# Half of the prompt's attention and output projection carried out inside the expert stage, with the second gather summed by token in column tiles

## The reference

```
mod = silu(c) @ w_ada + b_ada          -> shift, scale, gate, twice
h   = RMSNorm(x) * (1 + sc1) + sh1
q, k, v, p = split(h @ w_in)           # 512 features each
o_a = stick-breaking attention(q, k, v)    # 8 heads x 64, strictly causal
o_b = causal means over 2, 4, 8, 16 tokens of p, minus p, per-group map
x   = x + gt1 * RMSNorm(concat(RMSNorm(o_a), RMSNorm(o_b)) @ w_out)
h2  = RMSNorm(x) * (1 + sc2) + sh2
x   = x + gt2 * RMSNorm(PEER(h2))
PEER: per token and head (8 heads): two lists of 128 scores, the best 16
      of each, the best 16 of their 256 sums -> 16 of 16384 experts;
      sum over the 128 picks of gate * gelu(h2 . u_experts[i]) * v_experts[i]
```

## Time and profile before

| what | value |
|---|---|
| time, three runs | 3822.36, 3818.93, 3820.96 us |
| median | 3820.96 us |
| span of the profiled execution | 4199.6 us |
| mean granted clock of PE in it | 0.881 of full speed |
| expert stage in it | 904.6 to 4199.6 us |
| gathers | 2176 (1088 of each table) |

### The profile page before, as it was taken

How to read it: one execution, slowest core, us unless ns; L and a number is a source line. 1 busy time by engine, 2 the same in 40 slices (tenths; PEclk the granted TensorE clock), 3 DMA queues, 4 the chain that set the end, 5 groups by cost and what they waited for, 6 DMA issues and landing times.

```text
span 4199.6 us, 38180 instructions
## 1 busy us (share of the span) xinstructions
PE 3314.8 (79%) x9348; PEld 1593.5 (38%) x9348; DVE 2313.6 (55%) x5821; ACT 950.0 (23%) x2161; POOL 2152.0 (51%) x2222
## 2 busy tenths in 40 slices
PE   8998989928777777877777777777777777887677
PEld 2454555513333333333333333333333333333222
DVE  2104552867755665555665655566555665556442
ACT  1003773312221221112112211211121121112111
POOL 0000300236566665666666666566666665666665
PEclk9999999969898898898888888888888888888888
DMA  9104102159999999999999999899999999999997
GB/s 357 64 15 126 32 19 113 61 188 352 344 357 359 353 359 354 347 368 343 341 359 347 350 356 344 332 354 355 360 347 358 358 357 348 343 363 358 361 362 303
DMA packets 365168, 1245.51 MB, mean 297 GB/s; under 512 B 52129, under 2 KB 57505, under 8 KB 362751
## 3 DMA queue, kind: packets, MB, share of 16 engines
q0 software_dynamic: 313504, 1141.02, 72.4%
q1 hardware_dynamic: 48852, 96.77, 6.6%
q10 hardware_dynamic: 2576, 5.10, 0.4%
HBM read 1220.34 MB, written 22.39 MB: 296 GB/s over the span
## 4 chain that ended last, share of the span: by engine, by line
PE 38%; issue 17%; another core or an unknown queue 9%; DVE 5%; DMA 4%; POOL 3%; ACT 1%; DVEq 0%; POOLq 0%; ACTq 0%; SPq 0%
PE ps_y L1692 33%; PE ps_q L950 5%; DMA urow<-in_u_tab,idx 3%; POOL urow L1473 2%; POOL vrow L1473 1%; DMA vrow<-in_v_tab,idx 1%; DVE urow L1612 1%; ACT diag L1580 1%; DVE aux L993 0%; PE ps_s L961 0%; DVE i L996 0%; DVE sel L996 0%; DVE i L992 0%; DVE aux L1029 0%
## 5 line engine op out<-in xcount | busy, mean ns | idle before, releaser
L1692 PE MATMUL ps_y<-vrow,diag 128*128 128x512 f32 (+1 forms) x4352 | 2220.8, 665 | 647.5 <-issue 329.9
L1612 DVE CUSTOM_DVE_ANT_0 urow<-urow,ps_h 128x1024 f32<-128x1024 f32 x1088 | 1299.8, 1220 | 1025.2 <-DMA urow<-in_u_tab,idx 865.6
L1692 PEld LDWEIGHTS ps_y<-vrow,diag 128*128 128x128 f32 (+1 forms) x4352 | 884.3, 209 | 1893.6 <-issue 1576.9
L1473 POOL DMA_INDIRECT vrow<-in_v_tab,idx x1088 | 1031.6, 948 | 785.7 <-issue 287.4
L1473 POOL DMA_INDIRECT urow<-in_u_tab,idx x1088 | 1030.7, 947 | 430.5 <-issue 282.8
L1580 ACT ACTIVATE diag<-const,wgt 128x128 f32<-128x128 f32 x1024 | 373.1, 396 | 1766.2 <-PE ps_y L1692 643.3
L950 PE MATMUL ps_q<-aux,w_q_sb 128*128 128x128 f32 x2048 | 271.7, 292 | 58.1 <-issue 49.4
L950 PEld LDWEIGHTS ps_q<-aux,w_q_sb 128*128 128x128 f32 x2048 | 263.9, 207 | 94.4 <-issue 93.2
L1293 POOL TENSOR_TENSOR xo<-xo,ot 128x1024 f32<-128x1024 f32 (+1 forms) x9 | 21.1, 2343 | 352.2 <-DVE ot L1249 352.2
L530 PE MATMUL ps_z<-hT,w_in_sb 128*128 128x512 f32 (+1 forms) x576 | 190.5, 491 | 4.6 <-DVE hT L448 4.6
L625 POOL MEMSET kTs<- 128x384 f32 x1 | 0.4, 418 | 322.7 <-POOLq L344 322.7
(11 more groups left out here) (181 smaller groups left out, 2341.3 us busy)
## 6 DMA issues: line engine op xcount, KB each, us to landing
ada<-in_w_ada SPq DMA_DIRECT2D x12, 2048.0 KB, 12.5
urow<-in_u_tab,idx POOLq DMA_INDIRECT x1088
vrow<-in_v_tab,idx POOLq DMA_INDIRECT x1088
w_in_sb<-in_w_in SPq DMA_DIRECT2D x8, 1024.0 KB, 17.9
w_q_sb<-in_w_query SPq DMA_DIRECT2D x8, 1024.0 KB, 14.3
x<-in_x_p ACTq DMA_DIRECT2D x8, 512.0 KB, 6.6
w_out_sb<-in_w_out SPq DMA_DIRECT2D x8, 512.0 KB, 7.0
xo<-in_x_p SPq DMA_DIRECT2D x8, 512.0 KB, 3.7
```

The source lines that it names most:

```text
L1473: nc.gpsimd.indirect_dma_start(ring[k % RING][:, :], None, A[table][:, :], bass.IndirectOffsetOnAxis(ap=places[:, col:col + 1], axis=0)).t ...
L1612: nc.vector.tensor_tensor_reduce(out=urow[k % RING][:, :], in0=urow[k % RING][:, :], in1=ps_h[:, :], scale=1.0, scalar=0.0, op0=ALU.mult, ...
L1692: last = nc.tensor.matmul(ps_y[0:rows, c], diag[s % DIAGS][:, 0:rows], vrow[k % RING][:, c], start=(s == 0), stop=(s == PH * width(n) - 1))
```

## The change

The change does five things. The attention and output stages handle only queries and tokens 0 to 511 and the sample tokens: 11 units per pair and five tiles. The rest is in a class `Front`, cut into 102 "spots": 72 for attention (18 for each of four pairs: 16 units and two to drain the pipeline), then norms, eight products with halves of w_out, and ten for residual and second norm. A spot stands after a group of four picks in the expert stage on PE, ACT and DVE (`spot`; three a head in body 1, four a head in bodies 2 to 4, 14 of them in body 4), with its loads and stores on SP at the same place. Its tiles go through DRAM between the steps.

The v rows are gathered one token at a time (partition = pick, 128 picks of the token). Their indices and weights are transposed by PE. For four tokens, a "quad", ACT puts 128x4 weights into the middle column of four 63-column windows of zeros (`put`), and PE multiplies a 32-column view of each window with the token's rows, into 32 partitions of ps_y each (`quad`: eight products of 32x512). The v rows of a tile are gathered in the body after that of its u rows, so there are ten bodies. The first has u rows alone, the last v rows alone. The u ring has 6 buffers, the v ring 8, and POOL issues four u, then four v (two v in body 1). The search of a head is cut into 17 steps, one after each u product, and shares one PSUM bank with its queries. The bodies are unrolled.

```diff
-    for qc in range(2):
-        top = 4 * qc + 3
-        for kb in range(top, -1, -1):
-            c0 = max(0, kb * P - qc * 512)
-            for h in range(2):
-                units.append(dict(h=h, bank=qc, kb=kb, c0=c0, c1=512, first=kb == top, diag=kb >= 4 * qc,
-                                  last=kb == 0, opens=kb == top and h == 0, closes=kb == 0 and h == 1))
+    top = EARLY - 1
+    for kb in range(top, -1, -1):
+        for h in range(2):
+            units.append(dict(h=h, bank=0, kb=kb, c0=kb * P, c1=HALF, first=kb == top, diag=True,
+                              last=kb == 0, opens=kb == top and h == 0, closes=kb == 0 and h == 1))
     for kb in (2, 1, 0):
-        units.append(dict(h=2, bank=2, kb=kb, c0=0, c1=P, first=kb == 2, diag=kb == 2, last=kb == 0,
+        units.append(dict(h=2, bank=1, kb=kb, c0=0, c1=P, first=kb == 2, diag=kb == 2, last=kb == 0,
                           opens=kb == 2, closes=kb == 0))
...
+NU = NT + 1
+URING = 6
+VRING = 8
+ZRING = 4
...
-    tiles = TILES[-1:] + TILES[:-1]
+    tiles = TILES[-1:] + TILES[:EARLY]
...
-    heads = {2: [0], 3: [1], 4: [2], 5: [3], 6: [4], 7: [5], 8: [6, 7]}
...
+    PAIR, UNITS = 18, 16
+    ATT = 4 * PAIR
+    SQ = ATT + 1
+    OUT = (ATT + 8, ATT + 14)
+    POST = ATT + 20
+    END = POST + 10
...
+    def score(self, pe, m):
+        i, j, h, kb, diag, c0, lo = self.unit(m)
+        if m % self.UNITS == 0:
+            pe.wait_ge(self.kq_in, 32 * (i + 1))
+        if m >= 2:
+            pe.wait_ge(self.e_done, m - 1)
+        hr = slice(HD * h, HD * (h + 1))
+        self.nc.tensor.matmul(self.z[m % 2][:, c0:HALF], self.kT[hr, P * kb:P * (kb + 1)], self.q[hr, c0:HALF],
+                              start=True, stop=True, skip_group_check=True).then_inc(self.z_done, 1)
+    def after(self, pe, m):
+        i, j, h, kb, diag, c0, lo = self.unit(m)
+        z = self.z[m % 2]
+        pe.wait_ge(self.sp_done, m + 1)
+        last = self.nc.tensor.matmul(z[:, c0:HALF], self.ntri, self.sp[m % 2][:, c0:HALF], start=False, stop=True,
+                                     skip_group_check=True)
+        if j and lo < HALF:
+            last = self.nc.tensor.matmul(z[:, lo:HALF], self.nones, self.R[h][(j - 1) % 2][:, lo:HALF], start=False,
+                                         stop=True, skip_group_check=True)
+        last.then_inc(self.t_done, 1)
+    def values(self, pe, m):
+        i, j, h, kb, diag, c0, lo = self.unit(m)
+        if m % self.UNITS == 0:
+            pe.wait_ge(self.v_in, 16 * (i + 1))
+            if i:
+                pe.wait_ge(self.o_read, i)
+        pe.wait_ge(self.e_done, m + 1)
+        if diag:
+            pe.wait_ge(self.w_done, self.diags(m))
+        hr = slice(HD * h, HD * (h + 1))
+        self.nc.tensor.matmul(self.acc[hr, c0:HALF], self.v[:, kb, hr], self.w[m % 2][:, c0:HALF], start=(j == 0),
+                              stop=(kb == 0), skip_group_check=True).then_inc(self.pv_done, 1)
...
+    def logs(self, act, own, m):
+        i, j, h, kb, diag, c0, lo = self.unit(m)
+        nc, s = self.nc, self.sp[m % 2][:, c0:HALF]
+        act.wait_ge(self.z_done, m + 1)
+        if m >= 2:
+            act.wait_ge(self.t_done, m - 1)
+        own.link(nc.scalar.activation(s, self.z[m % 2][:, c0:HALF], ACT.Abs))
+        own.link(nc.scalar.activation(s, s, ACT.Exp, scale=-1.0))
+        nc.scalar.activation(s, s, ACT.Ln, bias=1.0).then_inc(self.l_done, 1)
...
+    def softplus(self, dve, own, m):
+        i, j, h, kb, diag, c0, lo = self.unit(m)
+        nc, s = self.nc, self.sp[m % 2]
+        own.wait()
+        dve.wait_ge(self.l_done, m + 1)
+        soft = nc.vector.scalar_tensor_tensor(out=s[:, c0:HALF], in0=self.z[m % 2][:, c0:HALF], scalar=0.0,
+                                              in1=s[:, c0:HALF], op0=ALU.max, op1=ALU.add)
+        if diag:
+            own.link(soft)
+            self.masked(s, c0).then_inc(self.sp_done, 1)
+        else:
+            soft.then_inc(self.sp_done, 1)
+        if kb:
+            dve.wait_ge(self.sp_done, m + 1)
+            if m >= 2:
+                dve.wait_ge(self.t_done, m - 1)
+            new, old = self.R[h][j % 2], self.R[h][(j - 1) % 2]
+            fresh = HALF if j == 0 else lo
+            if fresh > c0:
+                own.add(nc.vector.tensor_copy(new[:, c0:fresh], s[:, c0:fresh]))
+            if fresh < HALF:
+                own.add(nc.vector.tensor_tensor(new[:, fresh:HALF], old[:, fresh:HALF], s[:, fresh:HALF], ALU.add))
...
+        def spot(g, j):
+            if g < PH:
+                return None
+            if g < 2 * PH:
+                return 3 * (g - PH) + j - 1 if j else None
+            p = 3 * PH + 4 * (g - 2 * PH) + j
+            return p if p < front.END else None
...
         @block.gpsimd
...
-            def gather(table, ring, full, n, h, k):
-                col = width(n) * h + k
-                places = idx0 if is_sample(n) else idx
-                nc.gpsimd.indirect_dma_start(
-                    ring[k % RING][:, :], None, A[table][:, :],
-                    bass.IndirectOffsetOnAxis(ap=places[:, col:col + 1], axis=0)).then_inc(full[k % RING], 16)
...
-                    for k in range(TOPK):
-                        if ahead and k < width(un):
-                            pool.wait_ge(u_used, slots(un, uh) + (k - RING + 1))
-                            pool.sem_inc(pool_passed, 1)
-                            gather("u_tab", urow, u_full, un, uh, k)
-                        if k < width(n):
-                            if not (is_sample(n) and h == 0):
-                                pool.wait_ge(v_used, slots(n, h) + (k - RING + 1))
-                                pool.sem_inc(pool_passed, 1)
-                            gather("v_tab", vrow, v_full, n, h, k)
...
+            def gather_u(n, s):
+                k, at = u_slot(n, s) % URING, (find.idx0 if is_sample(n) else find.idx)[:, s:s + 1]
+                if s % width(n) == 0:
+                    pool.wait_ge(idx_ready, find.known(head(n, s // width(n))))
+                if u_slot(n, s) >= URING:
+                    pool.wait_ge(u_used, u_slot(n, s) - URING + 1)
+                nc.gpsimd.indirect_dma_start(urow[k][:, :], None, A["u_tab"][:, :],
+                                             bass.IndirectOffsetOnAxis(ap=at, axis=0)).then_inc(u_full[k], 16)
+            def gather_v(n, i):
+                t = token(n, i)
+                k, at = v_slot(n, i) % VRING, find.idxT[n % 2][:, t:t + 1]
+                if i == 0:
+                    pool.wait_ge(idxT_ready, n + 1)
+                if v_slot(n, i) >= VRING:
+                    pool.wait_ge(v_used, v_slot(n, i) - VRING + 1)
+                nc.gpsimd.indirect_dma_start(vrow[k][:, :], None, A["v_tab"][:, :],
+                                             bass.IndirectOffsetOnAxis(ap=at, axis=0)).then_inc(v_full[k], 16)
+            for b in range(BODIES):
+                nu = PH * width(b) if b < NU else 0
+                nv = rows(b - 1) if b else 0
+                for i in range(0, max(nu, nv), 4):
+                    each = 2 if b == 1 else 4
+                    for u in range(i, min(i + 4, nu)):
+                        gather_u(b, u)
+                    for v in range(i * each // 4, min(i * each // 4 + each, nv)):
+                        gather_v(b - 1, v)
...
-                            nc.scalar.activation(diag[s % DIAGS][:, :], ident, ACT.Copy, scale=weight)\
-                                .then_inc(diag_ready, 1)
...
+            def put(n, c):
+                q, j = n * QUADS + c, rows(n) // QUADS
+                if q >= ZRING:
+                    act.wait_ge(v_used, quad_end(q - ZRING))
+                nc.scalar.activation(place[:, q % ZRING, 0:j, MID],
+                                     wgtT[:, 0:rows(n)].rearrange("p (j c) -> p j c", j=j)[:, :, c], ACT.Copy)\
+                    .then_inc(placed, 1)
...
-                    un, uh = (n, h + 1) if h < PH - 1 else (n + 1, 0)
-                    if h < PH - 1 or more:
-                        products(un, uh)
-                    if h == 0:
-                        if not is_sample(n):
-                            finish(n - 1)
-                            find.search(own, dve, dve_passed, n, PH - 1)
-                    elif more:
-                        find.search(own, dve, dve_passed, n + 1, h - 1)
-                    if h < PH - 1 or more:
-                        weights(un, uh)
...
+            for b in range(NU):
+                w = width(b)
...
+                    g = head(b, h)
+                    early = 3 if h == 0 else 0
+                    if b and g + 2 < HEADS:
+                        for step in range(early):
+                            find.search(own, dve, g + 2, step)
+                    for k in range(w):
+                        product(b, h, k)
+                        if k == (1 if h == 0 else 2) and g:
+                            weights(g - 1)
```

(43 more changed lines are left out.)

1117 lines of the change are left out of this document (750 added, 367 removed).

## The result

The changed kernel takes 3875.66 us (median of four runs, 3868.83 to 3884.36) against 3821.66 us: 1.4% slower, ratio 1.0141 with a 95% interval of 1.0125 to 1.0158. The forecast was 3757, faster; the time lies inside the range, on the other side of zero, at the place that rival B gave (3880). The profiled span is 3872.7 us, 3 us from the median; the span of before, at 4199.6, had been 379 us above its median.

What follows compares the result with a forecast made beforehand. Gathers were taken to bound the expert stage, PE or its chains the stages before. Terms -225 + 60 + 14 + 25 + 10 + 15 + 10 + 27 = -64 took 3821 to 3757 us, range 3650 to 3900.

Steps and rivals of the forecast that it cites:

- rival B: Bodies 2 to 4 and last body: chain of waits starves gathers at 7.03 us a quad; 3978, middle 3880; chance 0.28.
- front: Stages before the experts: attention loses 16 units in four pairs, -170, output four tiles, -55; together -225 us.
- moved bytes, and what spots still hold up: Expert stage: 24.6 MB of moved attention and output transfers share full queues with the gathers at 410 GB/s, +60 us.
- body 1: Eight heads in the expert stage: DVE's 34.7 us a head against 30.7 of gathers, up to +32, taken as +25.
- spots of bodies 2 to 4, with output work: 72 attention spots at a period of 10.8 us, +10 for uneven arrival; output work among spots +15.
- last body: v rows alone, two quads in the ring: 11.9 us against 10.2 over 32 quads, +27, bounds 0 and 98.
- the signs that the prediction named: Softplus waiting over 2 us a spot for ACT, POOL behind u products: slower; front under 200 us or last body below 250 GB/s: wrong.
- ring of waits: Spots of bodies 2 to 4: DVE, POOL, PE and ACT wait in turn, 19.0 us and the quad for two groups.
- The quad, on which I let the outcome depend: Eight narrow products on PE, taken as 2.6 us between 1.75 and 7.03; the gain is gone at 3.8.
- Rival A: Expert stage stays gather-bound throughout, slack between 1.34 and 1.28 us a gather taking up small stalls: 3656 us; chance 0.18.
- Rival C: Expert stage's profiled dips are in timed runs too and come from the diagonals; quads bring 1.28 us a gather: 3625; chance 0.08.
- undisturbed pace of 1.28 us a gather: Expert stage of the kernel before: gathers at 1.28 us in an undisturbed stretch, timed runs at 1.34, 5% above.

Runs made afterwards that it cites:

- experiment 1: Changed kernel with a spot's work put ahead of the quad on PE and ahead of the weight copy on ACT: 3707.33 us, ratio 0.9702 to the kernel before.
- experiment 3: Changed kernel without spots and their transfers, tiles 5 to 8 taking h2 and x1 of tiles 1 to 4: 3631.68 us, ratio 0.9501 to the kernel before.
- experiment 4: Changed kernel with v rows going round twelve buffers in the last body, four of them from the u ring: 3823.24 us, ratio 1.0001 to the kernel before.
- experiment 8: Changed kernel with spots ahead of quad, twelve last-body v buffers, later gain products: 3659.56 us; with u and v gathered in turn besides: 3639.01 us.
- experiment 5: Kernel before with the last two of eight prompt tiles of the expert stage left out: 3140.68 us against 3819.53 on the same chip.
- experiment 2: Changed kernel with POOL issuing u and v gathers one by one in turn instead of in runs of four: 3726.98 us, ratio 0.9749 to the kernel before.

## Why the prediction was wrong

Step by step, forecast against measured:

| term | forecast, us | measured, us | from |
|---|---|---|---|
| front | -225 | -236 | first gather, 904.62 and 668.23 |
| moved bytes, and what spots still hold up | +60 | +71 | bodies 1 to 4, experiments 1 and 3 |
| body 0 | +14 | +11 | 95.2 against 64 x 1.32 |
| start of body 0 (gain rows) | 0 | +8 | first product behind first gather, 15.2 against 7.4 |
| body 1 | +25 | +73 | 341.6 against 268.5 in experiment 1 |
| spots of bodies 2 to 4, with output work | +10, +15 | +94 | 1166.4 against 1072.8 in experiment 1 |
| tile boundaries | +10 | -11 | eight tiles: bodies 5 to 7 at 338, before at 339.4 |
| last body | +27 | +53 | experiment 4 |

The measured terms sum to +63, the kernel lost 54. The 9 us between them I cannot place; the kernel before has its own start, sample tile and end, which none of the runs took apart. Of the signs that the prediction named, the waits spoke for B: DVE's softplus waited 215.4 us for ACT over 64 units, 3.4 us each, and POOL 493 us behind u products. The two that were to show it wrong did not appear: the front saved 236 us, and the last body's rate was 284 GB/s with the end.

*The step that failed is the price of the ring of waits.* Its links stood in the prediction in the right order, and each was taken at or near its best. The turn shown against the sum for two groups:

| link | forecast, us | measured, us |
|---|---|---|
| two products, then POOL's issue | 3.0 | 3.4 (1414.21 to 1417.57) |
| a u and four v issues, landing | 6.2 + 4.3 | 11.2 (to 1428.77) |
| quad | 2.6 | 3.3 (to 1432.06) |
| spot on PE | 2.65 | 4.1 (to 1436.13) |
| spot on ACT | 1.6 | 2.0 (to 1438.15) |
| spot on DVE | 1.2 | 1.3 (to 1439.49) |
| sum | 21.6 | 25.3 |

No link is far off. PE's two make 2.1 of the 3.7 us, for two reasons. The quad, granted a clock of 0.55, took 3.3 us, against 1.92 at 1.00; how much of the loss a full clock would return was not tried. The spot was granted 1.00, so the clock is not its reason: its four products are all 512 wide, and four such products took 3.44 us in the attention stage too, from this row to 447.69:

```profile
444.25 1.02 PE L713 MATMUL ps_s<-qz,kT 128*128 128x512 f32 x2
```

The 2.65 us that I took is the mean over 16 units, many of them narrower. The landing I took from a plain load, which makes 1.24 + 4.3 = 5.5 us from the start of an issue; the first gather of before was read 7.4 us after its issue (904.62 to 912.00), and the turn has 6.2. Both longer values could be read before the change. And even 21.6 for two groups is 10.8 a group, which is just the pace that I gave the gathers. A sum that has no slack at the best value of every link had to be forecast as binding; I wrote +10 for uneven arrival. Bodies 2 and 3 took 12.8 and 12.4 us a group (409.7 and 397.1 over 32), and 11.0 and 11.3 in experiment 1, with the ring loosened.

*Body 1* is the second failure: I priced it by DVE's work, 34.7 us a head, and never put it through the ring. With two v issues fewer, the prediction's own links give (21.6 - 2.5)/2 = 9.6 us a group, 38 a head, +60 for eight heads over the 30.7 of the gathers where I took +25; it took 42.7 a head. DVE's work is the same in experiment 1, which takes 268.5/8 = 33.6. *The last body* has the same two errors in small: two quads took 3814.97 - 3801.22 = 13.75 us where I had 11.9, with 6.3 us from the last issue (3808.71) to the quad and a quad of 3.22 to 3.50 us, at a clock of 0.53 to 0.59, instead of 2.6.

*The quad, on which I let the outcome depend, came near what I took.* I put it at 2.6 us between 1.75 and 7.03. It is 1.92 at a clock of 1.00, and the one at 0.55 took 3.29; the 32 quads of body 2 took 3.2 us on average:

```profile
1120.20:1529.90 409.70, 102.47 (x512) 20.28 (x512) 0.75 0.91 338
```

(The row is of the products at L2199 alone: length, busy us of PE and PEld, clock, DMA share, GB/s.) By the prediction's own price, 36 us in the spots for each microsecond, that is some 20 us, not the whole loss. So rival B came out in place, though its price, products that follow one another, did not: its point of decision, a quad of 3.8 us, was too high because the links around it were too short. That its 3880 lies 4 us from the result is luck. The trace shows how far column tiles overlap: 7.03/1.92 = 3.7 times for four, both lengths at a clock of 1.00. The four products of the spot shown, of which the first has weights 64 columns wide (128*64) and the last 64 rows deep (64*128), start 0.95 to 1.00 us apart at a clock of 1.00, where the full ones of the attention stage start 0.86 apart (3.44/4), also at 1.00; no run takes apart what makes the some 0.1 us a product.

*Rival A* was wrong for this kernel, but its sum fits the mended one: 3656 against 3659.56 and 3639.01 in experiment 8. *Rival C* is out by experiment 5: the prediction's reason not to believe the profiled dips held. Its undisturbed pace of 1.28 us a gather did not: no body of 256 gathers in these kernels runs below 1.30 (the shortest, of experiments 2 and 8, take 334.2 us), so the slack of 5% between 1.34 and 1.28 was hardly there. One reading was loose as well: the DMA digits of before are not 9 in all of the last 32 slices, which also have a 5, an 8 and a 7; nothing hangs on it.

## What to carry to other kernels

Work that is fitted into idle time of engines must be counted as a ring, not as busy shares: list which wait hands on to which across engines and buffers, and put it ahead of, not behind, the instruction that waits for a transfer, on every engine that it visits. Price each link at the clock and the queue of the stage where it will run, and for the widest unit, not the mean one. When a ring comes out equal to the pace of whatever bounds the stage, forecast it as binding. And take away the wait before adding a buffer: here two reordered calls gave 168 us, a seventh buffer 79.
